# Seven block products in place of eight in the middle down projections of a macaron encoder layer

## What is computed

```python
x = LN1(ALPHA*x + 0.5*swiglu(x, ffn1_w_up, ffn1_w_down))   # swiglu: a, b = split(x @ w_up); (silu(a)*b) @ w_down
h = mixer(x)      # one projection, short convolution, 4 retention heads, gates, w_out
x = LN2(ALPHA*x + h)
x = LN3(ALPHA*x + 0.5*swiglu(x, ffn2_w_up, ffn2_w_down))   # D_FF = 2816 = 22 tiles of 128
```

## Time and profile before

| | |
|---|---|
| median of 3 runs | 1780.93 us (1778.66 to 1781.36) |
| span of the profiled execution, the only time given for it | 1778.3 us |
| PE busy / DVE / ACT / POOL | 1766.5 / 1286.1 / 653.3 / 551.6 us |
| moved by DMA | 282.61 MB, 159 GB/s on average |

### The profile page before, as it was taken

How to read it: one execution, slowest core, us unless ns; L and a number is a source line. 1 busy time by engine, 2 the same in 40 slices (tenths; PEclk the granted TensorE clock), 3 DMA queues, 4 the chain that set the end, 5 groups by cost and what they waited for, 6 DMA issues and landing times.

```text
span 1778.3 us, 26857 instructions
## 1 busy us (share of the span) xinstructions
PE 1766.5 (99%) x10776; PEld 1653.0 (93%) x10776; DVE 1286.1 (72%) x1708; ACT 653.3 (37%) x1120; POOL 551.6 (31%) x355
## 2 busy tenths in 40 slices
PE   9999999999999999999999999999999999999998
PEld 9989999898999999999998989898989989899997
DVE  7958485678788787777266777767867968485676
ACT  5425233243545454444105050514224325242343
POOL 3424242242232222221242323332343324233331
PEclk9999999999999999999999999999999999999999
DMA  7442423334443333433674858676963442324223
GB/s 275 136 137 72 143 78 130 126 94 178 148 148 127 115 128 99 139 98 95 243 247 159 313 198 296 214 265 222 351 264 118 129 154 86 131 79 135 90 89 107
DMA packets 87259, 282.61 MB, mean 159 GB/s; under 512 B 8672, under 2 KB 9056, under 8 KB 86880
## 3 DMA queue, kind: packets, MB, share of 16 engines
q1 hardware_dynamic: 48096, 172.77, 29.4%
q10 hardware_dynamic: 24784, 56.21, 8.7%
q0 software_dynamic: 14256, 51.91, 8.6%
HBM read 239.63 MB, written 42.28 MB: 159 GB/s over the span
## 4 chain that ended last, share of the span: by engine, by line
PE 94%; DVE 3%; DMA 1%; ACT 1%; issue 1%; DVEq 0%; ACTq 0%
PE ps L872 93%; PE ps L1348 1%; DMA out_ret_sample<-state 1%; DMA state<-in_state_ret 0%; DVE xl L1961 0%; DVE z L2277 0%; DMA opening<-in_opening 0%; DVE z L2380 0%; PE ps L1257 0%; DVE wql L1961 0%; ACT xh L1510 0%; ACT t L1900 0%; DVE t L2010 0%; DVE y L2415 0%; DVE tl L1961 0%
## 5 line engine op out<-in xcount | busy, mean ns | idle before, releaser
L872 PE MATMUL ps<-th,wql 128*128 128x320 f32 x1136 | 351.0, 309 | 0.0
L872 PE MATMUL ps<-th,wqh 128*128 128x320 f32 x1136 | 350.7, 309 | 0.0
L872 PE MATMUL ps<-tl,wqh 128*128 128x320 f32 x1136 | 350.0, 308 | 0.0
L773 POOL TENSOR_TENSOR wl<-raw,wh 128x1024 fp32r<-128x1024 f32 x100 | 262.8, 2628 | 133.9 <-DMA wh<-in_weights 81.8
L1510 ACT ACTIVATE pu<-ps 128x320 f32<-128x320 f32 x213 | 93.2, 438 | 515.8 <-PE ps L872 515.8
L1961 DVE TENSOR_TENSOR wql<-qraw,wqh 128x512 fp32r<-128x512 f32 x213 | 260.0, 1221 | 17.2 <-ACT wqh L1510 17.0
L872 PE MATMUL ps<-xh,wql 128*128 128x320 f32 x852 | 262.7, 308 | 0.2 <-DVE wql L1961 0.2
L872 PE MATMUL ps<-xl,wqh 128*128 128x320 f32 x852 | 262.7, 308 | 0.0
L872 PE MATMUL ps<-xh,wqh 128*128 128x320 f32 x852 | 262.6, 308 | 0.0
L786 POOL TENSOR_TENSOR quad_s<-qraw 128x512 f32<-128x512 f32 x71 | 96.7, 1362 | 478.8 <-DVE wql L1961 412.9
L1961 DVE TENSOR_TENSOR wql<-quad_s,wqh 128x512 fp32r<-128x512 f32 (+1 forms) x213 | 197.5, 927 | 44.2 <-ACT wqh L1510 43.4
(11 more groups left out here) (246 smaller groups left out, 3446.2 us busy)
## 6 DMA issues: line engine op xcount, KB each, us to landing
qraw<-in_quads SPq DMA_DIRECT2D x142, 512.0 KB, 3.6
raw<-in_weights SPq DMA_DIRECT2D x100, 512.0 KB, 3.9
wh<-in_weights POOLq DMA_DIRECT2D x92, 512.0 KB, 5.3
state<-in_state_ret ACTq DMA_DIRECT2D x32, 512.0 KB, 7.5
out_ret_sample<-state ACTq DMA_DIRECT2D x32, 512.0 KB, 6.4
state<-in_state_ret SPq DMA_DIRECT2D x16, 512.0 KB, 5.7
qk_scratch<-ctp SPq DMA_DIRECT2D x8, 640.0 KB, 5.6
swish_scratch<-ctp SPq DMA_DIRECT2D x6, 640.0 KB, 2.9
```

Of the source, the lines that this page charges most:

```text
L773: pool.tensor_tensor(w_lo(r), w_raw(r), w_hi(r).bitcast(f32), ALU.subtract).then_inc(chunk_split, 1)
L872: ins = nc.tensor.matmul(out, lhs, rhs, start=start, stop=stop, skip_group_check=adds)
```

## The change

The down products of the eight middle groups are made by blocks. Of the five token tiles, 0 and 1 are set against 3 and 4; with two row blocks of 256 hidden rows and two halves of the output columns, seven block products (Winograd's form) take the place of eight. They use the sums n1, n2, t3, t4 of blocks of h, which DVE makes, ACT rounds and DVE splits, and four weight sums S1 = A21+A22, S2 = A11+S1, S3 = A11+A21, S4 = A12+S2 (A12: columns 0 to 511, hidden rows of the second block). Token tile 2 stays plain, in its right half as h0 S1 + (h1 - h0) A22, with the sum d (`df`). The weight sums are made in DRAM: ACT's queue copies four blocks (2 MB), POOL's queue adds two to them by an accumulating DMA (1 MB), then one for S2 and one for S4 (512 KB each). The chunks of a group are A11, S1, S2, A12, S3, A22, S4, seven in place of four. Bank roles are y, o1, x, o2, w; x is read out twice on the way, w and others more than once, 16 evacuations a group. The next quad's last low parts come behind them in DVE's queue. Slots go from three to four, and the reserve for GpSimd's DMA descriptors from its default to 2048 bytes a partition.

```diff
@@ -31,10 +31,14 @@
...
-NSPL = 3
+NSPL = 4
...
+SPLIT_GROUPS = range(1, len(GROUPS) - 1)
+SPLIT_CHUNKS = ("A11", "S1", "S2", "A12", "S3", "A22", "S4")
+SUMS_KEPT = ("S1", "S3", "S2", "S4")
+SPLIT_BANKS = 8
+FFN_CHUNKS = 4 + 2 + len(SPLIT_CHUNKS) * len(SPLIT_GROUPS) + 4
@@ -602,6 +665,14 @@
...
+        def chunk_source(engine, c):
+            if not is_sum(c):
+                return a["weights"][PLAIN[c]]
+            at, what = split_chunk(c)
+            engine.wait_ge(sums_added[{"S1": 0, "S3": 0, "S2": 1, "S4": 2}[what]], 16 * (at + 1))
+            return a["sums"][at, SUMS_KEPT.index(what)]
@@ -652,13 +723,21 @@
...
-                for g in range(1, len(GROUPS)):
+                for g in SPLIT_GROUPS:
+                    load(1)
+                    load_quad(2 * k)
+                    load_quad(2 * k)
+                    load(1)
+                    load_quad(2 * k)
                     load(2)
                     load_quad(2 * k)
-                    load(1)
-                    for _ in range(3):
-                        load_quad(2 * k)
-                    load(1)
+                    load(3)
@@ -772,6 +851,19 @@
...
+            def add_first(at):
+                pool.wait_ge(base_copied, 16 * (at + 1))
+                pool.dma_start(a["sums"][at, 0:2].rearrange("m p d -> (m p) d"),
+                               a["sum_add"][at].rearrange("m p d -> (m p) d"), accum_op=ALU.add,
+                               max_dma_last_dim=4 * D).then_inc(sums_added[0], 16)
+            def add_next(at, step):
+                pool.wait_ge(sums_added[step - 1], 16 * (at + 1))
+                pool.dma_start(a["sums"][at, step + 1], a["sums"][at, 0 if step == 1 else 2], accum_op=ALU.add,
+                               max_dma_last_dim=4 * D).then_inc(sums_added[step], 16)
@@ -816,21 +908,40 @@
...
-                for g in range(1, len(GROUPS)):
+                for g in SPLIT_GROUPS:
+                    at = split_after(k, g)
+                    high(ck(1))
+                    sums(2 * k)
+                    add_first(at)
+                    low()
+                    sums(2 * k)
+                    add_next(at, 1)
+                    high(ck(2))
+                    sums(2 * k)
+                    add_next(at, 2)
                     high(ck(3))
-                    for part in range(3):
-                        sums(2 * k)
-                        if (g, part) == (len(GROUPS) - 1, 2):
-                            pool.wait_ge(c22_made, QUAD_START[2 * k] + QUADS - 1)
-                        low()
-                    if (k, g) == (0, len(GROUPS) - 1):
-                        all_sums(1)
-                    else:
-                        sums(2 * k)
-                    if g == len(GROUPS) - 1:
-                        high(ck(1))
-                        pool.wait_ge(h_summed, PAIRS * (k + 1))
                     low()
+                    sums(2 * k)
+                    low()
+                    low()
+                    high(ck(2))
+                    low()
+                    high(ck(2))
+                    low()
+                    low()
@@ -1107,6 +1218,92 @@
...
+            def split_lead():
+                pe.wait_ge(h_ready, hr(2))
+                s, b0 = chunk(), bk.at
+                pe.wait_ge(psum_free, b0 + 3 - 7)
+                for kk in range(2):
+                    last = mm3(ps[:, (b0 + 3) % 8, :], (hh[:, kk, 0:128], hl[:, kk, 0:128]),
+                               (cols(kk, 512, w_hi(s)), cols(kk, 512, w_lo(s))), kk == 0, kk == 1)
+                last.then_inc(down_full, 1)
+                return s
+            def split_down(led, h0):
+                at, b0 = split_done.at, bk.at
+                y_at, o1, x_at, o2, w_at = (0, 1), 2, (3, 4), 5, (6, 7)
+                def product(s, place, left, start):
...
+                        pe.wait_ge(psum_free, b0 + place - 7)
+                    for kk in range(2):
+                        last = mm3(ps[:, (b0 + place) % 8, :], (left[0](kk), left[1](kk)),
+                                   (cols(kk, 512, w_hi(s)), cols(kk, 512, w_lo(s))), start and kk == 0, kk == 1,
+                                   adds=not start)
...
+                def read(n):
+                    pe.wait_ge(down_read, 8 * at + n)
...
+                product(led, x_at[1], of_h(0, 1), True).then_inc(down_full, 1)
+                product(led, o1, of_h(0, 2), True)
+                owed[0] = True
+                s = chunk()
+                summed(1)
+                for q in range(2):
+                    product(s, w_at[q], of_sum(n1h, n1l, q), True).then_inc(down_full, 1)
+                product(s, o2, of_h(0, 2), True)
+                owed[0] = True
+                s = chunk()
+                summed(2)
+                for q in range(2):
+                    read(1 + q)
+                    product(s, x_at[q], of_sum(n2h, n2l, q), False).then_inc(down_full, 1)
+                owed[0] = True
+                s = chunk()
+                pe.wait_ge(h_ready, h0 + 4)
+                for q in range(2):
+                    product(s, y_at[q], of_h(2, q), True).then_inc(down_full, 1)
+                product(s, o1, of_h(2, 2), False).then_inc(down_full, 1)
+                owed[0] = True
+                s = chunk()
+                summed(3)
+                for q in range(2):
+                    read(5 + q)
+                    product(s, x_at[q], of_sum(t3h, t3l, q), False).then_inc(down_full, 1)
+                owed[0] = True
+                s = chunk()
+                summed(5)
+                for q in range(2):
+                    read(7 + q)
+                    product(s, x_at[q], of_sum(t4h, t4l, q), False).then_inc(down_full, 1)
+                product(s, o2, of_sum(dh, dl, 0), False).then_inc(down_full, 1)
+                owed[0] = True
+                s = chunk()
+                for q in range(2):
+                    last = product(s, w_at[q], of_h(2, 3 + q), False)
+                    if q == 0:
+                        last.then_inc(down_full, 1)
+                last.then_inc(psum_full, SPLIT_BANKS)
+                owed[0] = True
+                bk.add(SPLIT_BANKS)
+                split_done.add()
@@ -1156,7 +1353,7 @@
...
-                    led = lead_down()
+                    led = split_lead() if split_quad(n) else lead_down()
@@ -1235,10 +1432,8 @@
...
-                    elif g < len(GROUPS) - 1:
-                        for half in range(2):
-                            natural(tiles // 2, hh, hl, lambda k: pe.wait_ge(h_ready, h0 + k + 1),
-                                    led=None if half else led)
+                    elif g in SPLIT_GROUPS:
+                        split_down(led, h0)
@@ -1611,6 +1806,29 @@
...
+            def base_copy(at):
+                if at:
+                    act.wait_ge(sums_added[0], 16 * at)
+                act.dma_start(a["sums"][at].rearrange("m p d -> (m p) d"),
+                              a["sum_base"][at].rearrange("m p d -> (m p) d")).then_inc(base_copied, 16)
+            def split_his(n):
+                ts_hi_part(n2h, n2f)
+                ts_hi_part(t3h[:, :, :], t3f[:, :, :])
+                ts_hi_part(dh[:, :, :], df[:, :, :])
+                act.wait_ge(h_ready, 2 * (stage_of(n) // 2 + 1) + 2 * (ffn_index(n) // 2 + 1))
+                ts_hi_part(t4h, t4f[:, :, :])
@@ -1622,6 +1840,8 @@
...
+                if split_quad(n) and local(n) % 4 == 2:
+                    ts_hi_part(n1h[:, :, :], n1f[:, :, :])
@@ -1644,16 +1864,22 @@
...
                     gate(n)
+                if ends and split_quad(n):
+                    split_his(n)
...
+                        if q == 2 and g in SPLIT_GROUPS and split_after(k, g) < 2 * len(SPLIT_GROUPS) - 1:
+                            base_copy(split_after(k, g) + 1)
@@ -2111,6 +2337,94 @@
...
+            def ts_lo_part(out, f, hi):
+                ts.add()
+                dve.wait_ge(ts_hi, ts())
+                tt(out, f, hi.bitcast(f32), ALU.subtract).then_inc(ts_ready, 1)
+            def first_difference(n):
+                dve.wait_ge(h_summed, ffn_index(n) // 2)
+                summed_of_h(tt(n1f[:, :, :], h32_first, h32_second, ALU.subtract))
+            def split_evacuations(n):
+                at = split_done.at
+                places = {"y0": 0, "y1": 1, "o1": 2, "x0": 3, "x1": 4, "o2": 5, "w0": 6, "w1": 7}
+                b0, seen, read = bk.at, Count(15 * at), Count(8 * at)
+                scale = 0.5 / ALPHA
+                def out_of(place, t, half, last, sign=1.0):
+                    if place == "w1" and last:
+                        dve.wait_ge(psum_full, b0 + SPLIT_BANKS)
...
+                    zt = cols(half, 512, z[:, t, :])
+                    ins = V.scalar_tensor_tensor(out=zt, in0=ps[:, (b0 + places[place]) % 8, :], scalar=sign * scale,
+                                                 in1=zt, op0=ALU.mult, op1=ALU.add)
+                    if last:
```

(67 more changed lines are left out.)

109 lines of the change are left out of this document (98 added, 11 removed).

## The result

The changed kernel takes 1881.96 us (median of 4 runs, 1876.23 to 1883.71) against 1780.22 for the kernel before on the same chip: ratio 1.0569, 95% interval 1.0552 to 1.0586. Slower was forecast, but by 58 us, not by 102, and the range ended at 1875.

The account below looks back on a forecast made before the run. TensorE (PE), busy for 99% of the span, was taken to bound the kernel. Waits of 10.0 us less 2.72 saved gave +7.3 a group, +58 in eight: span 1836, median 1839 us; range 1790 to 1875.

Parts of the forecast that it names:

- first mechanism: Down stretch: POOL's `low`s and DVE's two-SBUF-input operations exclude each other at shared ports; five `low`s cost DVE 9.7 us a group.
- Removed: Down products of a middle group: 108 matmuls in place of 120, saving 2.72 us a group, 21.8 in eight.
- n1 in the third quad: Third quad: 1.2 us more DVE work, covered by a POOL `low` that goes; taken as 0, up to 1.2 uncovered.
- Waits of the down stretch: Down stretch: PE waits for DVE's queue, 3.5 us before S2, 5.5 before S3, 1.0 before A22, 10.0 a group.
- Clock: Middle groups: granted clock read as 1.00 and matmul pace as 0.227 us; no term for a slower clock.
- The base copy has over 45 us: DRAM sums: the 2 MB copy, estimated at 15 us, has over 45 us to finish; cost taken as 0.
- The adds: DRAM sums: first add 10.8 to 16.8 us against 13.5 available; cost 0, or +24 us at the slow end.
- the hidden queue: Rival, down stretch: POOL's `low`s fall beside PSUM evacuations or yield to DVE, 1.1 us of waits, 1768 us; chance 0.14.
- the half collisions: Rival, down stretch: half the port collisions, 5.3 us of waits, net +2.6 a group, 1802 us; chance 0.17.
- The adds are slow: Rival, quads: slow DRAM adds make POOL late there besides, 1839 + 24 = 1863 us or more; chance 0.08.

Follow-up runs that it names:

- four corners: Changed kernel with weight sums in DRAM, POOL/DVE collisions, both or neither: neither 1759, DRAM sums alone 1809, collisions alone 1843, both 1882 us.

## Why the prediction was wrong

Its direction and first mechanism were right, its size was not, and the range did not hold the time. By its own steps:

- **Removed, 2.72 us a group.** Measured 2.56 (76.47 to 73.91): right.
- **n1 in the third quad, 0.** Right: without sums in DRAM and with short `low`s there is no wait.
- **Waits of the down stretch, 3.5 + 5.5 + 1.0 = 10.0.** Measured by itself as 9.1 with the clock held up (83.0 - 73.9, fill included), 1 us under the forecast: 2.9 before S2, 5.6 before S3, 0.6 before A22, counting fill and wait together. The collisions are shown to be the cause: with the `low`s cut short, nothing is left of it. In the changed kernel the same DVE queue shows as 1.1 + 4.9, because the wait before S1 comes first and covers S2's.
- **Clock: not in the sum.** This is the first step that failed. I took the pace of 0.227 us as fixed, from a trace in which PE never waits in a middle group, so that it couldn't show what the clock does behind a wait. Its net price is 11 us without the sums in DRAM. There the two errors nearly cancel, by luck: 1843 measured, 1839 forecast.
- **"The base copy has over 45 us", 0.** This is the step that failed most. It asked only whether the copy would be done in time, and so gave it no price; that it takes the 16 DMA engines from whatever is loaded beside it was not asked. The rows to ask it of were there: the quads' loads land after 3.6 us, and POOL begins the last quad's sum at 248.27, 3.5 us before the stretch:

```profile
248.27 1.29 POOL L786 TENSOR_TENSOR quad_s<-qraw 128x512 f32<-128x512 f32 x1 [4.66 <-DVE wql L1961]
```

With the copy alone that load was 4.0 us late and PE waited 2.0, so 2 us was all the slack. The copy itself landed in 10.0 us, sooner than my estimate of 15.
- **The adds, 0 with +24 at the slow end.** The first add landed in 9.6 (median; estimate 10.8 to 16.8), the second in 5.6 to 8.2, the third, where a copy ran beside it, in 12.8 to 14.8; POOL waited 48.5 us for adds in eight waits. Alone they cost the kernel before 10, within the bound. Bound and copy were taken one by one, though, and they cost most where they meet. Together they make 39 us (1882 against 1843), 49 in the kernel before.

In a sum: 1780 - 21 (matmuls) + 73 (collisions, 1832 - 1759) + 11 (clock) + 39 (sums in DRAM) = 1882. It closes because each term is the difference of two runs; the sums in DRAM cost 39 as the last term and 50 with the collisions away. The forecast had - 22, + 80, 0 and 0. Of the rivals, the hidden queue and the half collisions are out. "The adds are slow" came nearest in time; its place, POOL held up by adds inside the quads, is not where the large part lay: that was SP's load for the last quad, behind the copy and the third add.

Of the rules that bear on this, one would have given the question. The Trainium skill (DMA: Bandwidth & Descriptors, "Issuing engines are not separate DMA queues") says that DMAs issued from several engines save only the time of issuing, since the same DMA engines carry them. The copy was on ACT's queue, the load on SP's, and the trace agrees: 3.6 us became 8.8.

What stays open: what would be left of the cost if the third add waited until the last quad's load has landed, or the copy ran in slower pieces than 512 KB; neither was tried. Why the four corners give 11 us less together than one by one was not taken apart either; that waits cover each other, as S1's did S2's, is the likely reason, argued and not shown.

## What to carry to other kernels

Ask of every added transfer not only when it must be done but which load it runs beside, and how much slack the chain behind that load has; cost what meets in one place together. Where an engine never waits, its trace can't tell what its waits will cost: put a line for the clock behind every long wait (the shortest that lowered it here was 2.0 us, and two of 3.1 and 3.3 did not), and remember that slow matmuls ahead of another wait are paid already. VectorE's and GpSimd's shares of busy time, 45% and 19% in the stretch before, say nothing about work that must take turns.

## What the hardware showed

- In the middle groups of the changed kernel the granted clock fell behind PE's waits of 3.7 us and more and behind one of 2.7 (before S3, at 214.0), and stayed at 1.00 behind those up to 2.4 and the 3.1 and 3.3 of the last middle group; with the late copy and short `low`s it fell behind 2.0 (at 180.7). So the length of one wait doesn't settle it. Where it fell, 6 to 14 matmuls ran at the slower pace (0.427 us for 512 columns). After the 4.7 us wait of the changed kernel the pace was low at once, after the 2.7 us wait of the kernel without sums some matmuls ran at 0.227 first.
- A DRAM to DRAM copy of 2 MB took 8.7 to 11.8 us, and its packets had 91% of the engines' time for 6 us, at 380 GB/s. In the changed kernel the 512 KB quad loads issued beside it took 8.7 to 11.6 us in place of 3.6, the `wh` loads 13.6 to 15.6 (median before: 5.3). With more and smaller packets the copy took 15.5 us and its neighbours 7.7 to 10.3 and 12.4 to 14.8.
- An accumulating DMA of 1 MB took 9.3 to 11.4 us (medians), one of 512 KB 5.7 (median) alone with its like and 12.8 to 14.8 beside a copy.
